# The nine query tiles of the second layer's up-projection in another order

## What is computed

```python
# z = rmsnorm(h) @ b_w_in ; qa = first 384 columns, qm = last 256
qh = (rmsnorm(qa, b_q_norm) @ b_w_qb).reshape(b, t, 6, 128 + 64)
q_nope = qh[..., :128]                 # six heads, 128 wide
q_rope = rope(qh[..., 128:], pos)      # six heads, 64 wide, rotated
q_lat = einsum('bthn,hcn->bthc', q_nope, w_uk)
o_lat = mla_attend(q_lat, q_rope, c, kr, pos)
```

## Time and profile before

| what | value |
|---|---|
| median of three runs | 1654.03 us (1651.86 to 1656.52) |
| the profiled execution, its time | 1651.49 us |
| its span | 1649.7 us |
| mean granted TensorE clock | 0.97 |
| PE busy | 1547.9 us (94%) |
| DVE busy | 827.9 us (50%) |
| ACT busy | 565.6 us (34%) |
| POOL busy | 50.4 us (3%) |

### The profile page before, as it was taken

How to read it: one execution, slowest core, us unless ns; L and a number is a source line. 1 busy time by engine, 2 the same in 40 slices (tenths; PEclk the granted TensorE clock), 3 DMA queues, 4 the chain that set the end, 5 groups by cost and what they waited for, 6 DMA issues and landing times.

```text
span 1649.7 us, 28864 instructions
## 1 busy us (share of the span) xinstructions
PE 1547.9 (94%) x11443; PEld 1438.9 (87%) x11443; DVE 827.9 (50%) x1288; ACT 565.6 (34%) x876; POOL 50.4 (3%) x76
## 2 busy tenths in 40 slices
PE   3899999779999999999999789999899999999998
PEld 3889999569999999999988457766799999999998
DVE  4846777635533433334576645655454334343344
ACT  4532222323422313223443135555243223132234
POOL 1120000010000000000001000000000000000000
PEclk8999999889999999999999889999999999999999
DMA  6543333122232332222324303543122223323221
GB/s 193 167 141 92 92 92 92 56 82 77 77 90 77 90 88 78 82 83 77 90 80 120 107 11 93 145 121 99 46 83 70 84 81 89 87 76 89 76 89 58
DMA packets 229383, 149.34 MB, mean 91 GB/s; under 512 B 11121, under 2 KB 222466, under 8 KB 229282
## 3 DMA queue, kind: packets, MB, share of 16 engines
q1 hardware_dynamic: 218802, 122.57, 25.8%
q0 software_dynamic: 6032, 20.28, 4.1%
q10 hardware_dynamic: 4448, 5.11, 0.9%
HBM read 140.26 MB, written 7.68 MB: 90 GB/s over the span
## 4 chain that ended last, share of the span: by engine, by line
PE 72%; DVE 5%; ACT 2%; issue 1%; ACTq 0%; DVEq 0%
PE ps L572 57%; PE ps L1064 3%; PE ps L1022 2%; PE ps L1091 2%; PE ps L1005 1%; PE ps L932 1%; PE ps L967 1%; PE ps L968 1%; DVE t L1858 1%; DVE wl L1566 1%; DVE rstd L1585 1%; PE ps L935 1%; PE ps L962 1%; PE ps L1000 0%; ACT wh L1172 0%
## 5 line engine op out<-in xcount | busy, mean ns | idle before, releaser
L572 PE MATMUL ps<-xh,wh 128*128 128x288 f32 x1542 | 334.5, 299 | 15.1 <-DVE wl L1566 15.1
L572 PE MATMUL ps<-mh,wh 128*128 128x288 f32 (+1 forms) x1424 | 325.3, 297 | 17.0 <-DVE wl L1566 13.7
L572 PE MATMUL ps<-xh,wl 128*128 128x288 f32 x1542 | 329.7, 295 | 0.0
L572 PE MATMUL ps<-xl,wh 128*128 128x288 f32 x1542 | 329.5, 295 | 0.0
L572 PE MATMUL ps<-ml,wh 128*128 128x288 f32 (+1 forms) x1424 | 322.9, 296 | 0.0
L572 PE MATMUL ps<-mh,wl 128*128 128x288 f32 (+1 forms) x1424 | 322.8, 295 | 0.0
L1172 ACT ACTIVATE wh<-raw 128x1024 fp32r<-128x1024 f32 (+1 forms) x195 | 202.1, 1036 | 286.0 <-PE ps L572 268.3
L1566 DVE TENSOR_TENSOR wl<-raw,wh 128x1024 fp32r<-128x1024 f32 (+1 forms) x195 | 233.0, 1195 | 74.0 <-ACT wh L1172 72.7
L572 PEld LDWEIGHTS ps<-xh,wh 128*128 128x128 f32 x1542 | 248.3, 190 | 20.6 <-DVE wl L1566 17.3
L572 PEld LDWEIGHTS ps<-mh,wh 128*128 128x128 f32 x1424 | 237.5, 190 | 19.9 <-DVE wl L1566 14.5
L572 PEld LDWEIGHTS ps<-xl,wh 128*128 128x128 f32 x1542 | 248.6, 189 | 0.0
(11 more groups left out here) (290 smaller groups left out, 1341.7 us busy)
## 6 DMA issues: line engine op xcount, KB each, us to landing
raw<-in_w_up SPq DMA_DIRECT2D x64, 512.0 KB, 4.0
raw<-in_w_down SPq DMA_DIRECT2D x64, 512.0 KB, 3.6
pages<-in_cache_mla SPq DMA_DIRECT2D x128, 160.0 KB, 2.2
raw<-in_a_w_in SPq DMA_DIRECT2D x26, 512.0 KB, 3.8
memkc<-in_cache_mem_k POOLq DMA_DIRECT2D x16, 256.0 KB, 4.6
memvc<-in_cache_mem_v POOLq DMA_DIRECT2D x16, 256.0 KB, 5.7
raw<-in_a_w_out SPq DMA_DIRECT2D x8, 512.0 KB, 3.7
raw<-in_b_w_out SPq DMA_DIRECT2D x8, 512.0 KB, 3.7
```

The source lines that it names most:

```text
L572: last = mm(ps[:, 2 * (m % 2) + c, 0:n], w[:, s, kk, :], x(kk, col, n), start=(kk == 0 and nth == 0), stop=(kk == k - 1 and nth == 2))
```

## The change

A list `QB` says which tile stands at each of the nine positions. Positions 1, 4 and 6 are now the three rotary tiles; 0, 2, 3, 5, 7 and 8 are the plain ones. The order of all other steps between the positions stays, on every engine. The loads follow the same order: SP's two-DMA loads now stand at positions 1, 4 and 6, and the count of the semaphore that tells of loads follows them. PE and ACT run the same lines as before. No operation is added or removed.

```diff
+QB = [0, 6, 1, 2, 7, 3, 8, 4, 5]
...
             wq = t["b_w_qb"][0]
-            for h in range(H_MLA):
-                load(M_QB + h, wcols(wq, (NOPE + ROPE) * h, 3), k=3)
-            for j in range(H_MLA // 2):
-                m = M_QB + H_MLA + j
+            for n, j in enumerate(QB):
+                if j < H_MLA:
+                    load(M_QB + n, wcols(wq, (NOPE + ROPE) * j, 3), k=3)
+                    continue
+                m = M_QB + n
                 sp.wait_ge(wlo_ready, m - NRAW + 1)
-                for n in range(2):
-                    c = (NOPE + ROPE) * (2 * j + n) + NOPE
-                    sp.dma_start(raw[:, m % NRAW, 0:3, 64 * n:64 * n + 64],
+                for a in range(2):
+                    c = (NOPE + ROPE) * (2 * (j - H_MLA) + a) + NOPE
+                    sp.dma_start(raw[:, m % NRAW, 0:3, 64 * a:64 * a + 64],
                                  wq[:, c:c + 64].rearrange("(k p) n -> p k n", p=P)).then_inc(w_loaded[m % NRAW], 16)
...
-        double = {M_KV + 2} | {M_QB + H_MLA + j for j in range(H_MLA // 2)}
+        double = {M_KV + 2} | {M_QB + n for n, j in enumerate(QB) if j >= H_MLA}
...
             def qb_tile(n):
-                m = M_QB + n
+                m, j = M_QB + n, QB[n]
                 if n == 0:
                     invert(6, rqn[:, :])
                 if m + 1 < M_OUT[1]:
                     w_tail(m + 1)
-                if n < H_MLA:
-                    scaled(m, qn[:, n, :], rqn[:, :])
-                elif m < M_OUT[1]:
-                    rotary(m, ((qr[:, n - H_MLA, :], 0, P),), rqn[:, :], C[qr_ready])
+                if j < H_MLA:
+                    scaled(m, qn[:, j, :], rqn[:, :])
+                else:
+                    rotary(m, ((qr[:, j - H_MLA, :], 0, P),), rqn[:, :], C[qr_ready])
```

## The result

The changed kernel took 1656.97 us in the median of 14 runs (1654.57 to 1659.59), the kernel before 1653.88 us (1650.02 to 1656.68, 14 runs). The medians are 3.1 us apart. The ratio is 1.0023, with a 95% interval of 1.0014 to 1.0032: some 3.8 us slower. So the change costs 2 to 4 us. The forecast was 1653.1, so 0.9 us faster. The measured time lies above the prediction's own range (1650.2 to 1656) and inside its range for 8 in 10 (1649 to 1658). The loss is smaller than the 0.3% that the prediction called "no change", but with this many runs it is clear of noise. One execution of the kernel before, among those beside e1 to e4, took 2197.71 us at a mean clock of 0.65 and is in no ratio.

A forecast was written before the change was run, and what follows sets the result against it. DVE was taken to bound the last three, rotary tiles. Order 0.79 and full-speed start 3.05 gave -3.84 us, slow clock +2.9, sum -0.9: 1653.1 us; own range 1650.2 to 1656, 8 in 10 1649 to 1658.

The forecast's parts named there:

- The queue argument: In DVE's queue the split for tile n + 2 stands behind tile n's 5.53 us rotary eviction, so PE waits.
- The sum at full clock: Query-tile stage with the clock at 1.00 everywhere: 0.79 + 3.05 = 3.84 us faster, next stage starting at 929.97.
- The term for the clock: Slow PE clock behind the new gaps: two of them pay, 1.4 + 1.5 = 2.9 us lost.
- the 4.2 us gap: PE idle ahead of tile 6, behind position 4's rotary eviction: sure to slow the clock, priced at 1.4 us.
- the two short ones: PE's gaps of 2.55 us ahead of tile 3 and 2.6 ahead of tile 8: toss-ups, one taken at 1.5 us.
- The one of 2.0: PE's gap ahead of the next stage, from the sample rows' tail: probably too short to slow the clock, no cost.
- The gain from the old slow start: First two items behind the query tiles run at full speed rather than slow: 3.05 us won.
- The second rival: Every gap in the stage slows the clock and the next stage still starts slow: +3.6 us, 1657.6; chance 0.15.
- the 11.9 us: PE's waits in the old stage; a rival had rotary work covered by PE's tiles: -12 to -15, chance 0.06.
- the pages: Page loads start later; a rival had the attention loop wait for them: +5 to +10 us, chance 0.03.
- taken up by the attention loop: Rival: both gains are lost in the attention loop's own first waits, 0 us, 1654.0; chance 0.05.

The follow-up runs named there:

- e1: The changed kernel measured again, nothing altered, against the kernel before: ratio 1.0013 (1.0003 to 1.0023).
- e4: The changed kernel with the weights of tile n + 2 split inside the rotary eviction of tile n, against the kernel before: ratio 0.9956.
- e2: The changed kernel with 69 filler matmuls in PE's four waits, against the kernel before: ratio 0.9977 (0.9965 to 0.9990).
- e8: The kernel before, profiled once more unchanged: a single execution of 1650.71 us, stage 42.7 us, no ratio.
- e3: The kernel before with 69 filler matmuls in its own three waits, against the kernel before: ratio 0.9989 (0.9978 to 0.9999).
- e5: The changed kernel with the split inside the rotary eviction plus 26 filler matmuls in three waits, against the kernel before: ratio 1.0050.

## Why the prediction failed

- **The queue argument held.** The split behind the eviction gives gaps of 2.55, 4.2 and 2.6 us, and the sample rows' tail one of 2.0. Measured: 2.58, 4.24, 2.64 and 2.06. e4 shows the cause of the first three by removing it, and keeps the last.
- **The sum at full clock held.** 35.39 us from tile 2 to the next stage, e2 measured 35.24; 3.84 us in all, e2 measured 3.79 against the profile that the sum was made on (2.6 against e8), and 3.8 in the ratio.
- **The term for the clock failed.** "I take the 4.2 us gap and one of the two short ones, 1.4 + 1.5 = 2.9", and of the last gap: "The one of 2.0 is probably too short." In the profile all four paid. The first rotary eviction behind tile 3 began 1.35 us later than the sum without falls, the next by 1.56 more, the next stage by 1.33 more, and its first two items took 1.84 more than 4.66: 6.1 rather than 2.9. The single prices were near (1.5, 1.4, 1.5), their number was not. In e1 three gaps paid, 5.3 in all: nothing at tile 3, 2.06 at tile 6 (above the "at most 1.9" of the sum), 1.35 at tile 8 and 1.90 in the first two items. The largest error in both is the last gap, which was put at nothing as "probably too short".
- **The gain from the old slow start was too large.** The 3.05 us came from one profile. e8 has 1.89 and e3's ratio 1.8. The new kernel has a slow start of 1.84 of its own, behind a gap of 2.06 us rather than 5.82, where the forecast had none. So against e8 the slow start won nothing.
- **The second rival is what came.** I gave it 0.15 and +3.6 us. The profile of the changed kernel has its four falls and +2.2 us, e1 three falls, and the ratios say 2.2 to 3.8 us. That 3.6 is so near is in part luck: the rival's terms add up to 7.45 (1.5, 1.4, 1.5 and 3.05), measured were 6.1. The rows had not decided it. 2.51 us of idling had been enough, but behind the 2.86 us and behind the 2.65 us ahead of tile 8 the kernel before ran on at full clock (windows of PE in its first profile):

```profile
429.53:431.53 2.00, 2.00 (x15) 1.00 0.14 37
918.20:920.85 2.65, 2.65 (x18) 1.00 0.00 0
```

- **The rule behind it.** The Trainium skill, "TensorE: Matmul & The Clock Gate", section "HAM oscillation — how this bites in real kernels", tells of the transition being paid at every burst. The trace of the changed kernel agrees in that: four waits, four falls. The waits that the Trainium skill shows there are for DMA and take some 3 to 5 us. That waits of 2.06 to 2.64 us for DVE can do it too is shown here by the traces alone.
- The other rivals fell. Nothing of the 11.9 us was covered, the pages were in time (the attention loop's first wait is 4.71 us before and after), and the loss was not taken up by the attention loop.

## What to carry to other kernels

Before spreading slow evictions among fast tiles, look at what else stands in the evicting engine's queue behind them: here it was the preparation of the next tile's weights, and moving it into the eviction turned a loss of 0.1 to 0.2% into a gain of 0.3 to 0.4%. Count every gap that a new order opens on TensorE, not only the idle time in total: one long gap pays the slow clock once, four short ones up to four times. And when a small insertion makes a far-off loop slower, look at the instruction packets and at the "issue" waits at the loop's restart before blaming what the insertion does in its own place.

## What was not expected of the hardware

- Idling as short as 0.49 and 1.08 us, with two transposes between, was followed by a fall of the clock in e4 and not in e11, and the 2.58 us gap fell in one profile of the changed kernel and not in the other. Near these lengths a gap had no fixed price; one profile is one draw.
- Matmuls whose result nobody reads can be worth their place: 69 of them took the changed kernel from 1.0013 (e1, beside the same runs of the kernel before) or 1.0023 to 0.9977, and 36 transposes in one wait go with 6.4 us less behind it. 26 of them in e5 made the kernel slower.
- Additional PE instructions ahead of a loop changed its speed: 26 more matmuls in a wait gave 1.0079 for the kernel before, with 30 instruction packets rather than 12 or 13. 69 more (e3) gave 0.9989 and 12 packets.
